# Two mixture-of-experts layers: three experts with fixed places in the first, and an earlier release of the weight buffers

## The reference, cut to what matters

```python
N_EXPERTS = 64; TOP_K = 8; EXPERT_DIM = 256; D_MODEL = 1024

def moe_ffn(h, w_router, e_bias, w_gate, w_up, w_down, s_gate, s_up, s_down):
    scores = jax.nn.sigmoid((h @ w_router).astype(jnp.float32))
    _, idx = jax.lax.top_k(scores + e_bias, TOP_K)      # 8 of 64 experts for each token
    wts = jnp.take_along_axis(scores, idx, axis=-1)
    wts = wts / wts.sum(-1, keepdims=True) * ROUTE_SCALE
    ...
    # for each expert e and the tokens xb that chose it:
    a = jax.nn.silu(xb @ w_gate[e]) * (xb @ w_up[e])
    y = a @ w_down[e]                                   # weighted and added to the token's row
    ...
    shared = (jax.nn.silu(h @ s_gate) * (h @ s_up)) @ s_down
    return routed + shared
```

## Time and profile before

| what | us |
|---|---|
| median of 3 runs (3669.88 to 3679.59) | 3678.89 |
| the profiled execution, its time | 3669.65 |
| the profiled execution, its span | 3667.9 |
| rounds of the first layer (first gate product to the load of the sums) | 2069.98 to 2774.96 |
| rounds of the second layer (first to last gate product) | 3087.15 to 3618.50 |
| PE busy over the span | 3331.9 (91%) |

### The profile page before, as it was taken

One profiled execution on the slowest core, in us unless ns is written; L12 is line 12 of the kernel. 1 busy time (PEld: TensorE's weight loads), 2 busy tenths in 40 slices (PEclk: granted clock), 3 DMA queues, 4 the chain that ended last, 5 costly groups with the idle time before them and its releaser, 6 DMA issues.

```text
span 3667.9 us, 40285 instructions
## 1 busy us (share of the span) xinstructions
PE 3331.9 (91%) x14420; PEld 2243.3 (61%) x14420; DVE 1382.3 (38%) x3103; ACT 536.2 (15%) x1122; POOL 401.7 (11%) x455
## 2 busy tenths in 40 slices
PE   7799989999999999899998988999995998999997
PEld 4688877888888887778564433444343675333333
DVE  5566525555025664665353322222213033111112
ACT  2210112001011003100132111111111022111111
POOL 0000011001010000000113111211112002000000
PEclk8899999999999999999998999999997999999999
DMA  7477533774436762565200689999992215999984
GB/s 285 185 300 297 218 115 146 298 269 154 154 115 243 285 228 94 192 235 214 75 29 0 221 287 389 376 357 357 351 363 84 80 69 217 369 409 367 417 363 178
DMA packets 136451, 860.80 MB, mean 235 GB/s; under 512 B 21712, under 2 KB 25168, under 8 KB 38736
## 3 DMA queue, kind: packets, MB, share of 16 engines
q1 hardware_dynamic: 94992, 672.18, 46.8%
q0 software_dynamic: 40560, 185.13, 14.7%
q10 hardware_dynamic: 720, 1.13, 0.1%
HBM read 849.95 MB, written 36.18 MB: 242 GB/s over the span
## 4 chain that ended last, share of the span: by engine, by line
PE 71%; DMA 14%; DVE 8%; issue 4%; ACT 1%; SPq 1%; POOL 0%; POOLq 0%; DVEq 0%; ACTq 0%
PE ps L745 15%; PE ps L1102 11%; PE ps L1341 10%; DMA ring<-stream_in 9%; PE ps L1083 8%; PE ps L841 7%; PE ps L1363 6%; DMA arena<-mod_stream_in 3%; PE ps L1379 3%; DVE arena L1852 2%; PE ps L1310 2%; DMA moe_out<-arena,slot_token 1%; PE ps L1278 1%; PE ps L757 1%; PE ps L800 1%
## 5 line engine op out<-in xcount | busy, mean ns | idle before, releaser
L1341 PE MATMUL ps<-ring,arena 128*64 128x512 f32 (+2 forms) x2112 | 611.4, 623 | 76.9 <-DMA ring<-stream_in 76.8
L1341 PEld LDWEIGHTS ps<-ring,arena 128*64 128x64 f32 (+2 forms) x2112 | 221.9, 156 | 407.2 <-issue 405.2
L1852 DVE SCALAR_TENSOR_TENSOR arena<-arena,cond 128x512 f32<-128x512 f32 x602 | 426.5, 748 | 84.3 <-DMA arena<-mod_stream_in 75.3
L1102 PE MATMUL ps<-arena,ring 128*128 128x256 f32 x2048 | 451.9, 383 | 3.7 <-DVE arena L2168 3.7
L1102 PEld LDWEIGHTS ps<-arena,ring 128*128 128x128 f32 x2048 | 393.0, 193 | 58.5 <-issue 4.4
L1083 PE MATMUL ps<-H,ring 128*128 128x256 f32 x1920 | 421.9, 380 | 0.2
L1083 PEld LDWEIGHTS ps<-H,ring 128*128 128x128 f32 x1920 | 363.9, 191 | 50.1 <-issue 1.6
L1363 PE MATMUL ps<-ring,arena 128*64 128x512 f32 (+2 forms) x1056 | 309.7, 600 | 19.1 <-DMA ring<-stream_in 11.7
L1520 ACT ACTIVATE arena<-ps 128x512 f32<-128x512 f32 (+2 forms) x358 | 182.1, 509 | 828.3 <-PE ps L745 326.5
L2373 DVE TENSOR_TENSOR arena<-arena,ps 128x256 f32<-128x256 f32 x83 | 34.9, 421 | 646.3 <-ACT arena L1743 646.3
L1363 PEld LDWEIGHTS ps<-ring,arena 128*64 128x64 f32 (+2 forms) x1056 | 103.6, 150 | 193.7 <-issue 173.3
(11 more groups left out here) (275 smaller groups left out, 3280.0 us busy)
## 6 DMA issues: line engine op xcount, KB each, us to landing
ring<-stream_in SPq DMA_DIRECT2D x618, 1024.0 KB, 9.2
arena<-mod_stream_in POOLq DMA_DIRECT2D x124, 1024.0 KB, 5.1
YS<-mod_stream_in SPq DMA_DIRECT2D x12, 1024.0 KB, 4.8
arena<-mod_stream_in SPq DMA_DIRECT2D x8, 1024.0 KB, 13.1
moe_out<-zeros POOLq DMA_DIRECT2D x10, 256.0 KB, 5.7
moe_in<-YS POOLq DMA_DIRECT2D x1, 2048.0 KB, 9.4
moe_out<-arena POOLq DMA_DIRECT2D x1, 2048.0 KB, 8.2
YS<-moe_out POOLq DMA_DIRECT2D x1, 2048.0 KB, 18.4
```

Of the source, the lines that this page charges most:

```text
L1102: m = mm(out[:, i * T:(i + 1) * T], w[:, c * P:(c + 1) * P], f_h[:, 16 * half + c, :], start=(half == c == 0), stop=(half == 1 and c == 15))
L1341: m = mm(out[at, :], e_xt[:, k % 2, 4 * part + c, at], w[:, c * TC:(c + 1) * TC], start=(part == c == 0), stop=(part == 1 and c == 3))
L1852: ins = stt(acc, w, x, acc, MUL, ADD)
```

## The change

In the first layer experts 0, 1 and 2 take ranks 0 to 2 whatever their counts, in solo rounds, and the other 61 are sorted behind them. The two blocks `three_for_two` move from ranks 0 and 2 to ranks 3 and 5. Three solo rounds come ahead of them and three fewer stand at the end. The loads of the fixed experts name their pieces without the sort. In both layers a slot is released by the last product that uses it, with one exception: the last rank of parts 1 and 2, whose last product already signals the bank that it filled; that slot goes on the list `done` as before.

```diff
+FIXED = [3, 0]
 def moe_rounds():
-    first = three_for_two(0) + pair(32) + pair(34) + three_for_two(2) + pair(36) + pair(38)
+    first = solo(0) + solo(1) + solo(2) + three_for_two(3) + pair(32) + pair(34) + three_for_two(5) + pair(36) + pair(38)
     for i in range(12):
-        first += solo(4 + 2 * i) + solo(5 + 2 * i) + pair(40 + 2 * i)
-    for r in range(28, 32):
-        first += solo(r)
+        first += solo(7 + 2 * i) + solo(8 + 2 * i) + pair(40 + 2 * i)
+    first += solo(31)
...
             def experts(l):
-                sp.wait_ge(ordered, l + 1)
+                asked = False
                 for j, (r, part) in enumerate(MOE[l].order):
                     p = first + j
+                    if r < FIXED[l]:
+                        sp.wait_ge(piece_used[p % SLOTS], p // SLOTS)
+                        sp.dma_start(ring[:, p % SLOTS, :], stream[first + 3 * r + part]).then_inc(piece_full[p % SLOTS], 16)
+                        continue
+                    if not asked:
+                        sp.wait_ge(ordered, l + 1)
+                        asked = True
...
-                    done.extend(piece_used[(ph.first + j) % SLOTS] for j in plan_.freed[k, part])
                     return views
+                def used_up(k, part, r, m):
+                    if plan_.last[r, part] == k:
+                        free = piece_used[(ph.first + plan_.order.index((r, part))) % SLOTS]
+                        if part and r == rounds[k].ranks[-1]:
+                            done.append(free)
+                        else:
+                            m.then_inc(free, 1)
...
                                 if c < 3:
                                     freeing(m)
+                                else:
+                                    used_up(k, part, r, m)
...
                             if c == 0:
                                 freeing(m)
+                            elif half:
+                                used_up(k, 2, r, m)
...
                 stt(by_expert[...], ...).then_inc(drained[b], 1)
+                link(ts(o_spread[:, 0, :], ones, o_mine, None, MUL))
+                if FIXED[l]:
+                    for i in range(FIXED[l]):
+                        link(v.memset(o_key[:, i:i + 1], float(4 * TC * EXPERTS - i)))
+                    link(stt(o_rest, o_key, 1.0, o_twice, MUL, MUL, accum_out=o_mine))
                 link(stt(o_rest, o_key, o_mine, ones[:, 0:EXPERTS], ALU.is_ge, MUL, accum_out=o_place))
-                ts(o_spread[:, 0, :], ones, o_mine, None, MUL)
```

More of the change, by code:

```diff
@@ L259, in __init__ @@
         self.order, last = [], {}
-        for at, (k, part) in enumerate(steps):
+        for k, part in steps:
             for r in rounds[k].ranks:
@@ L263, in __init__ @@
                     self.order.append((r, part))
-                last[r, part] = at
-        self.freed = {step: [self.order.index(w) for w in self.order if last[w] == at - 1] for at, step in enumerate(steps)}
+                last[r, part] = k
+        self.last = last
         self.cap = [max(rd.first + P // len(rd.ranks) for rd in rounds if r in rd.ranks) for r in range(EXPERTS)]
         assert sorted(self.order) == [(r, part) for r in range(EXPERTS) for part in range(3)]
+FIXED = [3, 0]
 def three_for_two(r):
@@ L293, in spare_blocks @@
 def spare_blocks(l):
-    rows, caps = (TC, T)[l], MOE[l].cap
+    rows, caps, fixed = (TC, T)[l], MOE[l].cap, FIXED[l]
     best = {(0, 0): 0}
-    for r in reversed(range(EXPERTS)):
+    for r in reversed(range(fixed, EXPERTS)):
         grown = {}
@@ L303, in spare_blocks @@
                 total = used + count
-                if count <= rows and total + count * r <= rows * TOP_K:
+                if count <= rows and total + count * (r - fixed) <= rows * TOP_K:
                     got = blocks + max(0, -(-(count - caps[r]) // P))
@@ L308, in spare_blocks @@
         best = grown
-    return max(best.values())
+    return max(best.values()) + sum(-(-(rows - caps[r]) // P) for r in range(fixed))
 MOE = moe_rounds()
@@ L2275, in sort_experts @@
                 while r < EXPERTS:
-                    n = len([c for c in cap[r:] if c == cap[r]])
+                    n = next((i for i, c in enumerate(cap[r:]) if c != cap[r]), EXPERTS - r)
                     last = v.memset(o_caps[:, r:r + n], float(EXPERTS * cap[r]))
```

## The result

| what | before | after |
|---|---|---|
| median, us (runs side by side) | 3675.0 (3669.88 to 3679.59, 5 runs) | 3649.79 (3648.44 to 3656.16, 5 runs) |
| the profiled execution, time / span | 3669.65 / 3667.9 | 3649.79 / 3648.1 |
| first layer, first gate product to the load of the sums | 705.0 | 702.6 |
| second layer, start of the first to start of the last gate step | 524.3 | 508.1 |

The ratio is 0.9937 with the interval 0.9923 to 0.9951: the change is faster. The medians differ by 25.2 us, the profiled executions by 19.9, and the interval spans 18 to 28. The prediction said 3656 in a range of 3638 to 3673. Of the profiled 19.8 us of span, 16.2 lie in the second layer's rounds and 2.4 in the first layer's; the rest is small shifts elsewhere, 0.7 of them ahead of the first round.

A forecast was written before the change was run, and what follows sets the result against it. Slots, not bytes, were taken to bound the second layer's quads. First layer -2.6 and second -15.3 made -17.9: 3651.8 from the profiled 3669.65, 3661.0 from the median; forecast the middle, 3656, range 3638 to 3673.

The forecast's parts named there:

- The bound of the second layer: Second layer's quads: PE waits for slots, and earlier release removes 15.3 of 23.3 us, bounds -9.6 and -23.3.
- the clock after the waits: Second layer's quads: a shorter wait may spare the clock's fall, up to 1.8 us per quad, left out of the sum.
- Earlier release in the first layer: Four pair rounds behind the two blocks: slots released sooner, -2.5 us, bounds 0 and -6.
- Three solos in front: First layer: three solo rounds ahead of the blocks start the first pair round 34.9 us later, at 2138.9.
- first pair rounds: First layer: one gate piece instead of two in the ring ahead of the block's end, +1.5 us, bounds 0 and +6.0.
- lighter last group: First layer's last solo, solo, pair: no gathers beside it any more, -2.7 us, bounds 0 and -4.
- lane: End of the first layer: the last scatter lands behind the lane's load, +1.1 us, bounds -4.8 and +7.0.
- Together 0: First layer: three solo rounds more in front, +34.9 us, and three fewer behind, -34.87, cancel.
- Early loads pay: Rival, first layer: five pieces loaded ahead of the sort save 13.3 us where bytes bound, giving 3643; chance 0.12.
- Bytes bound the second layer: Rival: rounds between quads run at the DMA engines' pace, giving back some 5 us: 3661; chance 0.17.
- The spare block: Rival, behind the last round: an expert over 64 tokens adds a block of about 38 us: 3694; chance 0.05.
- It doesn't do what it says: Rival, second layer: last ranks' unchanged release holds the quads, giving 3662; counted within the 0.17 of the bytes rival.

The follow-up runs named there:

- e1: The changed kernel with the old order of rounds and no fixed experts, so only the earlier release in both layers; ratio 0.9912 to before.
- e3: The changed kernel, but SP waits for the sort before the first expert's load, so no expert is loaded ahead of it; ratio 0.9940 to before.
- r5: e1 with slots on the list also released by first transposes of rows and hidden rows and by the sums' first products; ratio 0.9920 to before.
- r6: The changed kernel with the gathers of rounds 2 and 3 issued ahead of the 2 MB store of the shared expert's output; ratio 0.9926 to before.
- r9: The changed kernel without fixed experts, so the three largest run into three spare blocks behind the last round; 3721.41 us in a single execution.
- e2: The changed kernel with the old release of slots, so only the fixed experts and the new order of rounds; ratio 1.0008 to before.
- k3: e1 with the earlier release in the second layer only, the first layer's slots freed as before; 3660.46 us, ratio 0.9962 to before.
- k4: The changed kernel with the gathers of rounds 2 and 3 ahead of the store and the lane's load behind its round's scatter; ratio 0.9920 to before.
- k1: e1 with the gathers of rounds 2 and 3 ahead of the 2 MB store; ratio 0.9916 to before.
- r8: e1 with more places of release, the gathers of rounds 2 and 3 ahead of the store, and the lane's load behind its round's scatter; 3639.34 us, ratio 0.9908.

## Why the prediction was right, and where its sizes were off

**The bound of the second layer: right, and undersized.** The wait there was one for slots. Predicted were waits of 2.65 in place of 5.85 and no down waits; measured 2.50 and 2.49 at two of the three quads, 5.22 at the other, and no down waits. The term was -15.3. The stretch measured -16.2 in the changed kernel's profile, and that nearness is partly luck: the waits for the ring fell by 13.1, less than the term, PE's whole idle time by 13.6, and 2.6 came from faster products, which the sum had left out. It measured -19.2 to -19.8 where the second quad has no extra wait (e1, e3, r5, r6, r9). The whole stretch in one line, before and e1 (us, PE busy, granted clock, DMA share, GB/s):

```profile
3087.15:3611.48 524.33, 498.84 (x2165) 0.98 0.94 384
```

```profile
3081.71:3586.57 504.86, 495.37 (x2164) 0.99 0.98 400
```

The idle part falls from 25.5 to 9.5 us: 16.0, for which the term said 15.3. The other 3.5 are in PE's busy time: the same products run faster, at a granted clock of 0.99 instead of 0.98. That is the clock after the waits (up to 1.8 us for each quad), which the prediction named and left out of the sum. It isn't a matter of the wait's length alone: in the changed kernel 2.50 was followed by 5.34 us and 2.49 by 3.64. The Trainium skill (TensorE: Matmul & The Clock Gate, HAM oscillation) describes a kernel whose products start at the lower clock after each DMA wait of some 3 to 5 us; here the row with 2.50 and 5.34 agrees, though its wait is shorter, and the row with 2.49 and 3.64 doesn't.

**Earlier release in the first layer: the step that was mis-sized.** The prediction took -2.5, for which it showed no working, with -6 as the bound. It measured -8.9 (e2 to after) and -8.8 (before to e1), outside the bound, and k3 puts it back; in the new order other pairs of profiles give as little as 3. The mechanism was the right one, priced too low: even the bound let only two steps save a third of a wait of 7.14, plus 1. In fact (k3 against e1) each of the four gate waits in the three pair rounds behind the blocks loses 1.7 to 3.0 us. How much of this is part 0's release and how much the down slots', these runs don't tell.

**Three solos in front, first pair rounds, lighter last group, lane: the sum was too low.** They were 0 + 1.5 - 2.7 + 1.1 = -0.1. After against e1, which has the same release, they are: solos 35.18 - 33.71 = +1.5, B +2.3, T -0.4, E -1.0, and F +1.4, which no term had: 3.7 in all in the first layer.

*Solos and first pair rounds.* With the new release three solos take 33.6 or 33.7 behind (34.87 and 35.86 with the old one), in front 35.2 to 35.6 with either: the release helps behind and not in front, so the prediction's "Together 0" was wrong by some 1.5. B's +2.3 is for the first pair rounds, predicted +1.5 in bounds of 0 to +6; over all profiles with the release the new order's B is 116.0 to 122.6 against 112.6 to 115.1, means 4.9 apart, so the price is probably nearer 5 than 1.5.

*Last group and last scatter.* The lighter last group came out as priced: 36.25 us against e1's 38.81, -2.6 for the -2.7 of the sum (35.2 to 37.0 in all profiles of the new order, 37.1 to 40.3 in those of the old). But the eleven groups ahead of it took 2.1 longer, so T fell by only 0.4 in this pair of profiles (2.5 in k4 against k1). The last scatter let POOL go on after 15.0 us, between the bounds of 11.32 and 23.15 and nearer the lower. The prediction let the rule of turns between queues (the Trainium skill, DMA: Bandwidth & Descriptors, Queues, rings and completion order) stand for its upper end. The rule isn't refuted by the lower number, because its premise was missing: the lane and the scatter are both in the profile's one software queue, which moved 2.35 MB in both stretches, but SP's pieces, in the hardware queue, brought 6.69 MB in the 23.15 us of the earlier trace rows and 0.40 MB in these 15.00. How the time splits between the lane and the pieces was not tested.

*F.* This stretch, with the gather of round 2 behind the 2 MB store, was 3.8 longer than in the earlier trace rows; in e1 and r5, in the old order, it was 2.5 and 3.9 longer, so this is for the most part a draw of each execution. A part may still be the order's: with the store in front the new order's F is 26.0 to 26.6 in all five profiles, the old one's 22.2 to 26.1 in four. It isn't the early loads', which e3 and r9 don't have (26.6).

**So the first layer's -2.6 against a measured -2.4 is agreement by accident.** A release worth -8.8 met some +6 from the order and from F. The second layer carried the forecast, and the last 1.2 us of the span's 19.8 lie outside both and were in no term.

**The rivals.** *Early loads pay* is out: e2, with them and without the release, is at 1.0008, and e3, without them, at 0.9940 against 0.9937. *Bytes bound the second layer* is out: the DMA share around the first quad rose from 0.64 to 0.91 and nothing came back later: the pair rounds between the quads take 15.86 us in both kernels. *The spare block* didn't occur (83 gathers as before); its price, 38 in series, is near what one alone would take by r9's rows. *It doesn't do what it says* is out: the quads wait 2.5 though their last rank keeps the old release, and r5, which releases that slot sooner too, shows no gain over e1.

**What stays open.** The second quad waits 5.22 in the changed kernel and 2.85 in e1. SP's issue of the piece is not late (1.2 us after part 0's start at both quads); from issue to landing (us, min/median/max), the second quad's piece and below it those of the first:

```profile
DMA to landing us min/median/max: 7.5/7.5/7.5
```

```profile
DMA to landing us min/median/max: 4.8/5.2/5.7
```

From the second quad's gate to the next round's it takes 22.7 to 23.2 us in the profiles of the changed kernel and of k1 to k4, 19.6 to 20.0 in those of e1, e3, r5, r6 and r9, and 17.1 in r8's. Both orders stand on both sides, so it isn't the change. The k kernels ran on the same chip as r5, r6, r8 and r9, so it isn't the chip alone. It is worth some 3 us of the second layer; k1 and k3 lose 3 more at their third quad. The DMA engines were busy with SP's pieces all the while (share 1.04 from 3334 to 3336.5); why this one landed late wasn't found.

## What to carry to other kernels

Signal that a buffer is free with the last instruction that reads it, not with the first of the next step: where the next step waits for a refill of that very buffer, the release waits with it, and the wait appears as one for DMA. A queue that stands 100 us before a sort costs little when nobody misses its pieces (here at most a few us, none of it shown); look for who waits on the ring, in single rounds, before you reorder work to feed it sooner. Price such a release at every step that waits, not only where the largest wait is: here four waits of 3 to 7 us in three pair rounds of the first layer gave 9 us beside the second layer's 19. And read a stage of a few us from several profiles: B differs by 6 us between kernels that are alike there.

## What the runs showed of the hardware

- A load of 1 MB landed 4.8 us after its issue at the first quad, and 7.5 us after it at the second.
- After waits of 2.5 us the same products took 3.64 us at a granted clock of 1.00, or 5.34 at 0.68, so a wait of this length may cost 1.7 us of clock or nothing.
- Behind the 2 MB load a scatter landed after 13.8 us at a DMA share of 0.54 and after 22.1 at 0.99; POOL's next issue came 15.00 and 23.15 us after the scatter's, and 11.27 with the load behind the scatter.
